# Two transformer blocks in one kernel: the first projections of the neighbourhood attention behind the last state product

## The chip, the cores and the metric

The kernel runs on one core of one Trainium2 chip. The metric is the device time of one execution in microseconds (us), the median of several runs. Besides it there is one profiled execution, from which all rows below come.

## What is computed

The reference runs two different transformer blocks in turn on 256 tokens of width 1024. Each has two layers. In the first block a layer mixes tokens by three branches: a latent attention (mla), a gated linear attention (gla) and a neighbourhood attention (na). Its input is 256 tokens and 256 context tokens. In the first layer context tokens are also given out, so all 512 tokens pass through; in the second only 256 outputs are needed, though keys and values of all 512 are.

```python
def hybrid_layer(h, hc, ...):
    z = modulate(rms_norm(h, norm1_w), sh1, sc1) @ w_in
    zc = modulate(rms_norm(hc, norm1_w), csh1, csc1) @ w_in
    a, bb, cc, gates = split_cols(z, GROUP_SPLITS)
    ya, ya_c = mla_mixer(a, a_c, ...)
    yb, yb_c = gla_mixer(bb, bb_c, ...)
    yc, yc_c = na_mixer(cc, cc_c, na_rpb, need_ctx_out)
    h = h + g1 * merge_branches(ya, yb, yc, gates, w_a_o, w_b_o, w_c_o, w_out)
    h = h + g2 * swiglu(...)

def gla_mixer(...):
    ...
    def finish(o, g):
        o = rms_norm(o.transpose(0, 2, 1, 3), norm_w)
        b, l = o.shape[0], o.shape[1]
        return o.reshape(b, l, GLA_V_W).astype(g.dtype) * jax.nn.silu(g)
```

The three branches read the same normed input. So the projections of the neighbourhood attention don't depend on what the linear attention gives.

## The kernel before

The program is written engine by engine. Each of TensorE (`pe`), ScalarE (`act`), VectorE (`dve`), GpSimd (`pool`) and SyncE (`sp`, which starts the transfers) has its own list of instructions, by hand, and semaphores between them. `x_done.at(label)` is the count of engine x at which a step with that label is over. `stage(...)` at the head of a part makes an engine wait until all four have ended the part before.

**Matmuls.** Matrices are kept as a high and a low part, and a product is three matmuls (high by high, high by low, low by high). `three`, lines 566 to 568, does it for projections that give features by tokens; `v_part`, lines 1213 to 1215, gives tokens by features.

**Weight panels.** All weights go through the same three raw buffers, in one fixed order, as panels of up to 128 x 2048. For each panel SyncE loads `raw` (line 516). `step(p)` prepares panel p + 2: ScalarE copies it to the high part `whi` (534); then VectorE takes the low part `wlo` of 5/8 of the columns and GpSimd that of the rest (543). `open_panel` on TensorE waits for all three, and `panel_used` counts the panels that TensorE is through with. A raw buffer is free for the next transfer once both low parts are made. In layer 0 panels of the modulation weights `w_mod` go through the same raw buffers. They aren't split; TensorE multiplies them as they are (line 770), and the last 17 of them stand in the neighbourhood attention of layer 0.

**The linear attention's end.** It runs over 8 chunks of 64 tokens, forward and then backward. In each step VectorE updates the state (2407), and TensorE makes an outer product (1158) and the product with the state (1190), which adds into the output in banks 0 to 3. OT is the number of token blocks of 128 that are given out, 4 in layer 0 and 2 in layer 1. In the backward pass the first 2 x OT steps also hold a gate product each (745 to 747). Ahead of these steps VectorE masks the products within a chunk (2393). ScalarE takes the silu of the gates (1803). After the last product with the state it squares the output and sums each head (1811), and takes the root (1814). VectorE inverts it (2413), norms (2417), multiplies with the gate (2422). TensorE turns each token block by four matmuls with the identity (894), and VectorE copies it to `y` (2423). The turned blocks use banks 6 and 7 in turn.

**The neighbourhood attention's beginning.** Panel 0 holds queries and keys of two heads (48 matmuls with up to 512 columns), panel 1 the values of four heads (96 matmuls with 256 columns, four token blocks). Then an attention loop over heads and query blocks starts with the score products (1237). The other projections are cut into parts, called fills, and laid into its steps by `na_plan`. SyncE loads a bias table `nbias` in 12 transfers (2895), GpSimd masks it in four operations (2775, 2778), and VectorE adds it to the scores (2142) and takes their maximum (2156). In the program of before, the bias transfers wait for the end of the linear attention on all four engines, and stand ahead of panel 2 in SyncE's list. GpSimd masks ahead of its share of panels 2 and 3.

## Time and profile before

| what | us |
|---|---|
| median of 3 runs | 3116.35 |
| lowest, highest | 3114.63, 3122.04 |
| the profiled execution | 3119.45 |
| its span, first to last instruction | 3117.7 |
| TensorE busy, matmuls | 2812.8 (90%) |
| mean granted TensorE clock | 0.951 |

TensorE is the busiest engine by far; VectorE is busy for 44% of the span, ScalarE for 39%, GpSimd for 36%. A share of the whole span says little about one seam between two stages, though: what counts there is who waits for whom, in order of time. The granted clock is a share of full speed: 1.00 is 2.4 GHz, 0.50 is 1.2 GHz.

### The profile page before, as it was taken

How to read it: one execution, taken by the hardware profiler on the slowest of the kernel's cores; microseconds unless marked ns; L12 is line 12 of the kernel's file. 1: busy time of each engine (PE TensorE's matmuls, PEld its weight loads, DVE VectorE, ACT ScalarE, POOL GpSimd, SP SyncE). 2: the span in 40 equal slices, each digit the busy share in tenths (PEclk: the TensorE clock that was granted, in tenths of full speed). 3: DMA queues.
4: the chain of work that ended last, by engine and by line, in shares of the span. 5: the costliest groups of instructions: out<-in, count | busy, mean ns of one | idle time of the engine just before them, and what ended most of it. 6: DMA issues, size and time to landing. Idle time of an engine off the chain costs nothing. (4 is left out here: it accounts for less than half of the span.)

```text
span 3117.7 us, 52810 instructions
## 1 busy us (share of the span) xinstructions
PE 2812.8 (90%) x20541; PEld 2502.8 (80%) x20541; DVE 1359.5 (44%) x2405; ACT 1217.7 (39%) x1791; POOL 1117.6 (36%) x457
## 2 busy tenths in 40 slices
PE   6789879799889999888789899899889999988998
PEld 4557667588779999566679799899779989977898
DVE  2443533332343433444434543534564353456433
ACT  2322223333244444422345444444444444444443
POOL 0101020132235565111214455354425555632453
PEclk8899989899989999998999999999999999989999
DMA  5454034533336666211415566465225646622563
GB/s 173 131 180 147 14 83 127 156 91 104 94 109 192 188 194 191 83 29 41 88 48 152 164 197 189 141 198 165 95 82 162 188 138 197 190 84 68 149 186 97
DMA packets 570660, 413.54 MB, mean 133 GB/s; under 512 B 36566, under 2 KB 548252, under 8 KB 570524
## 3 DMA queue, kind: packets, MB, share of 16 engines
q1 hardware_dynamic: 570524, 411.69, 44.6%
q8 instruction: 91, 1.49, 0.2%
q14 instruction: 45, 0.37, 0.0%
HBM read 410.58 MB, written 2.88 MB: 133 GB/s over the span
## 5 line engine op out<-in xcount | busy, mean ns | idle before, releaser
L543 POOL TENSOR_TENSOR wlo<-raw,whi 128x768 fp32r<-128x768 f32 (+2 forms) x353 | 1020.3, 2894 | 1701.6 <-ACT whi L534 1701.2
L566 PE MATMUL psum<-xh_n,whi 128*128 128x256 f32 (+1 forms) x3208 | 932.3, 291 | 79.6 <-DVE rtmp L2612 21.7
L567 PE MATMUL psum<-xl_n,whi 128*128 128x256 f32 (+1 forms) x3208 | 915.1, 285 | 0.0
L568 PE MATMUL psum<-xh_n,wlo 128*128 128x256 f32 (+1 forms) x3208 | 914.7, 285 | 0.0
L543 DVE TENSOR_TENSOR wlo<-raw,whi 128x1280 fp32r<-128x1280 f32 (+2 forms) x353 | 531.2, 1505 | 665.3 <-ACT whi L534 665.1
L534 ACT ACTIVATE whi<-raw 128x2048 fp32r<-128x2048 f32 (+2 forms) x353 | 643.2, 1823 | 396.0 <-PE psum L925 171.8
L566 PEld LDWEIGHTS psum<-xh_n,whi 128*128 128x128 f32 x3208 | 615.4, 192 | 114.4 <-issue 57.7
L568 PEld LDWEIGHTS psum<-xh_n,wlo 128*128 128x128 f32 x3208 | 617.3, 192 | 5.5
L567 PEld LDWEIGHTS psum<-xl_n,whi 128*128 128x128 f32 x3208 | 616.4, 192 | 4.7
L923 PE MATMUL psum<-hidh,whi 128*128 128x256 f32 x1232 | 344.0, 279 | 7.0 <-issue 7.0
L925 PE MATMUL psum<-hidh,wlo 128*128 128x256 f32 x1232 | 343.6, 279 | 0.0
L924 PE MATMUL psum<-hidl,whi 128*128 128x256 f32 x1232 | 343.6, 279 | 0.0
L923 PEld LDWEIGHTS psum<-hidh,whi 128*128 128x128 f32 x1232 | 234.1, 190 | 7.5 <-issue 7.5
L925 PEld LDWEIGHTS psum<-hidh,wlo 128*128 128x128 f32 x1232 | 234.7, 191 | 0.0
L924 PEld LDWEIGHTS psum<-hidl,whi 128*128 128x128 f32 x1232 | 234.1, 190 | 0.0
L1653 ACT ACTIVATE sg<-psum 128x256 f32<-128x256 f32 x154 | 59.2, 385 | 420.5 <-PE psum L568 420.4
L2201 DVE TENSOR_TENSOR hidf<-sg,psum 128x256 f32<-128x256 f32 x154 | 64.8, 421 | 259.9 <-ACT sg L1653 259.7
L566 PE MATMUL psum<-xh,whi 128*128 128x512 f32 (+1 forms) x360 | 146.1, 406 | 23.2 <-ACT whi L534 19.9
L567 PE MATMUL psum<-xl,whi 128*128 128x512 f32 (+1 forms) x360 | 143.3, 398 | 0.0
L568 PE MATMUL psum<-xh,wlo 128*128 128x512 f32 (+1 forms) x360 | 142.8, 397 | 0.0
L566 PEld LDWEIGHTS psum<-xh,whi 128*128 128x128 f32 (+1 forms) x360 | 68.9, 191 | 44.5 <-issue 19.0
L2203 DVE TENSOR_TENSOR hidl<-hidf,hidh 128x256 fp32r<-128x256 f32 x154 | 70.6, 458 | 74.6 <-ACT hidh L1655 74.6
(337 smaller groups left out, 3804.3 us busy)
## 6 DMA issues: line engine op xcount, KB each, us to landing
raw<-in_ffn_w_in SPq DMA_DIRECT2D x176, 512.0 KB
raw<-in_w_in SPq DMA_DIRECT2D x136, 512.0 KB
raw<-in_w_ffn_in SPq DMA_DIRECT2D x132, 512.0 KB
raw<-in_w_mod SPq DMA_DIRECT2D x96, 512.0 KB
raw<-in_ffn_w_out SPq DMA_DIRECT2D x88, 512.0 KB
raw<-in_w_ffn_out SPq DMA_DIRECT2D x66, 512.0 KB
raw<-in_w_out SPq DMA_DIRECT2D x32, 512.0 KB
raw<-in_w_a_o SPq DMA_DIRECT2D x16, 256.0 KB
```

The costliest lines, as they stand in the source:

```text
L534: act.activation(whi[slot][:, 0:size], raw[r % 3][:, 0:size], ACT.Copy).then_inc(hi_ready, 1)
L543: eng.tensor_tensor(wlo[slot][:, c0:c1], raw[raw_at[p0] % 3][:, c0:c1], whi[slot][:, c0:c1].bitcast(F32), ALU.subtract).then_inc(sem_, 1)
L566: pe.matmul(dst, sh, mh, start=start and n == 0, stop=False, skip_group_check=True)
L567: pe.matmul(dst, sh, ml, start=False, stop=False, skip_group_check=True)
L568: last = pe.matmul(dst, sl, mh, start=False, stop=n == len(pairs) - 1, skip_group_check=True)
L923: pe.matmul(dst, hi[:, w0:w0 + P], hidh[:, s_, j, :], start=False, stop=False, skip_group_check=True)
L924: pe.matmul(dst, hi[:, w0:w0 + P], hidl[:, s_, j, :], start=False, stop=False, skip_group_check=True)
L925: m = pe.matmul(dst, lo[:, w0:w0 + P], hidh[:, s_, j, :], start=False, stop=False, skip_group_check=True)
L1653: act.activation(sg[:, c, :], bank[4 + c][:, 0:S], ACT.Silu).then_inc(silu_done, 1)
L2201: dve.tensor_tensor(hidf[:, c, :], sg[:, c, :], bank[4 + c][:, S:2 * S], ALU.mult).then_inc(hid_done, 1)
L2203: dve.tensor_tensor(hidl[:, s_, c, :], hidf[:, c, :], hidh[:, s_, c, :].bitcast(F32), ALU.subtract).then_inc(hid_lo, 1)
```

## The change

It moves work at the seam between the linear and the neighbourhood attention, in both layers. No matmul is added or left out.

- TensorE: panel 0 (queries and keys, now into banks 4 and 5) stands directly behind the last state product. Then token blocks 0 and 1 of the linear attention's output are turned, then comes token block 0 of the values, then the other output blocks are turned, and then value blocks 1 to 3. The values go to banks 0 to 3, so each waits until the output in its bank is normed. The `stage` wait between the two attentions is gone on all engines.
- ScalarE: the high part of panel 0 is made ahead of the silus, that of panel 1 between the silus and the squares, and that of panel 3 behind the first value block.
- VectorE: its share of panel 0 stands behind the fourth state update of the backward pass, that of panel 1 behind the last. The key copy stands ahead of panel 2's share.
- GpSimd: its share of panel 2 stands ahead of the bias masks.
- SyncE: the transfer of panel 2 stands ahead of the bias transfers, which now wait only for the last state product.
- Memory: `nbias` lies behind what the linear attention still uses, `gst` has a place of its own, and the other small tiles are laid so that they cover only what is dead.

```diff
@@ memory
-        gst, o = at(o, "gst", [P, 16])
+        gst, _ = at(scratch + 33 * 1024, "gst", [P, 16])
...
-        nbias, o = at(o, "nbias", [P, HEADS, 6, 64])
...
+        nbias, o = at(scratch + 34 * 1024, "nbias", [P, HEADS, 6, 64])
@@ TensorE
-                pe.wait_ge(*act_done.at((tg, "silu", OT - 1)))
-                turn_y((tg, "y"), range(OT), lambda i: gv[:, i, :])
-                end("pe", tg)
...
-                stage(pe, "pe", tg, ("gla", l))
...
+                def v_head(t):
+
+                    if t < OT:
+                        pe.wait_ge(*dve_done.at((of_gla, "gn", t)))
+                    m = v_part(p0 + 1, t, 0, 8, bank[t][:, 0:S])
...
+                open_panel(pe, p0)
+                qk_part(p0, 0, slice(0, TM), 0, 8, bank[4][:, 0:TM]).then_inc(*pe_done.tick((tg, "mm", "q", 0)))
+                qk_part(p0, 1, slice(0, T), 0, 8, bank[5]).then_inc(panel_used, 1)
+                pe.wait_ge(*act_done.at((of_gla, "silu", OT - 1)))
+                turn_y((of_gla, "y"), (0, 1), lambda i: gv[:, i, :])
+                open_panel(pe, p0 + 1)
+                v_head(0)
+                turn_y((of_gla, "y"), range(2, OT), lambda i: gv[:, i, :])
+                end("pe", of_gla)
+                for t in range(1, 4):
+                    v_head(t)
@@ GpSimd
+                step(p0)
                 pool.wait_ge(*bias_loaded.at(("bias", l)))
-                pool.wait_ge(lo_ready_pool, p0 + 2)
+                pool.wait_ge(lo_ready_pool, p0 + 3)
...
-                for j in range(6):
+                for j in range(1, 6):
                     step(p0 + j)
@@ SyncE
-                for s_ in (pe_done, act_done, dve_done, pool_done):
-                    sp.wait_ge(*s_.at(("end", ("gla", l))))
+                sp.wait_ge(*pe_done.at(((("gla", l), "b"), "from state", 7)))
...
-                before[base["na", l] + 2] = [lambda l=l: bias_loads(l)]
+                before[base["na", l] + 3] = [lambda l=l: bias_loads(l)]
```

On TensorE, at the seam of layer 0, the program of before has this (`whi_54` and `wlo_57` are panel 0's parts, `whi_52` and `wlo_55` panel 1's):

```order
1023 L1190 MATMUL psum<-state,qdec 64x256 x2
1024 L894 MATMUL psum<-cst,gv 128x128 x16
1025 L566 MATMUL psum<-xh,whi_54 128x512
...
1073 L1213 MATMUL psum<-whi_52,xh 128x256
...
1169 L1237 MATMUL psum<-nk,nq 128x512 x2
```

and the changed one this:

```order
1023 L1190 MATMUL psum<-state,qdec 64x256 x2
1024 L566 MATMUL psum<-xh,whi_54 128x512
...
1072 L894 MATMUL psum<-cst,gv 128x128 x8
1073 L1209 MATMUL psum<-whi_52,xh 128x256
...
1097 L894 MATMUL psum<-cst,gv 128x128 x8
1098 L1209 MATMUL psum<-whi_52,xh 128x256
...
1170 L1243 MATMUL psum<-nk,nq 128x512 x2
```

The 16 turning matmuls (line 894) stood ahead of both panels; now eight stand behind panel 0 and eight behind the first value block.

On ScalarE at the same place, before (`whi_53` is panel 2's high part, and the later `whi_54` panel 3's):

```order
113 L1797 ACTIVATE kend<-psum 128x256 x4
114 L1803 ACT_TABLE_LOAD
115 L1803 ACTIVATE la<-psum 128x512 x4
116 L1811 ACTIVATE expc,gst<-psum 128x128 x16
117 L1814 ACT_TABLE_LOAD
118 L1814 ACTIVATE gst<-gst,eps 128x16
119 L534 ACTIVATE whi_54<-raw_49 128x2048
120 L534 ACTIVATE whi_52<-raw_50 128x2048
121 L534 ACTIVATE whi_53<-raw_51 128x2048
122 L1829 ACTIVATE nq<-psum 128x512
```

and now:

```order
113 L1803 ACTIVATE kend<-psum 128x256 x4
114 L534 ACTIVATE whi_54<-raw_49 128x2048
115 L1810 ACT_TABLE_LOAD
116 L1810 ACTIVATE la<-psum 128x512 x4
117 L534 ACTIVATE whi_52<-raw_50 128x2048
118 L1819 ACTIVATE expc,gst<-psum 128x128 x16
119 L1822 ACT_TABLE_LOAD
120 L1822 ACTIVATE gst<-gst,eps 128x16
121 L1834 ACTIVATE nq<-psum 128x512
122 L534 ACTIVATE whi_53<-raw_51 128x2048
```

Panel 0's high part moved ahead of the silus, panel 1's between silus and squares, and panel 2's behind the query copy.

On VectorE the changed program has, from the masked copies on:

```order
275 L2399 COPY_PREDICATED attm<-cst,psum 128x2x128 x8
276 L2413 SCALAR_TENSOR_TENSOR state<-state,expc,psum 64x128 x16
277 L543 TENSOR_TENSOR wlo_57<-raw_49,whi_54 128x1280
278 L2413 SCALAR_TENSOR_TENSOR state<-state,expc,psum 64x128 x12
279 L543 TENSOR_TENSOR wlo_55<-raw_50,whi_52 128x1280
280 L2422 RECIPROCAL gst<-gst 128x16
```

Before, the 28 state operations stood in one row, and both low parts behind the last copy of the turned output.

## Rows read from the trace of the kernel before

**Rows 1.** The page: the span, and GpSimd's share of a panel's low part.

```profile
span 3117.7 us, 52810 instructions
...
L543 POOL TENSOR_TENSOR wlo<-raw,whi 128x768 fp32r<-128x768 f32 (+2 forms) x353 | 1020.3, 2894 | 1701.6 <-ACT whi L534 1701.2
```

**Rows 2.** Busy time by stretch, layer 0: PE, PEld, DVE, ACT, POOL, clock, DMA, GB/s.

```profile
380.00:416.20 36.20, 36.20 (x286) 30.11 (x284) 9.70 (x28) 2.39 (x4) 0.00 (x0) 1.00 0.00 1
416.20:436.00 19.80, 4.14 (x17) 3.00 (x16) 12.36 (x27) 9.77 (x36) 4.26 (x2) 0.58 0.00 0
436.00:448.70 12.70, 12.66 (x48) 10.38 (x49) 1.19 (x1) 0.00 (x0) 1.71 (x1) 0.85 1.21 194
```

**Rows 3.** TensorE's waits, 416.2 to 461: total us, times, longest.

```profile
PE psum L894 <- DVE gv L2422: 9.8, 2, 8.7
PE psum L894 <- DVE y L2423: 3.6, 1, 3.6
PE psum L566 <- DVE wlo L543: 2.4, 1, 2.4
```

**Rows 4.** Order of time, seam of layer 0: start, us, instruction [idle before <-releaser].

```profile
415.12 1.08 PE L1190 MATMUL psum<-state,qdec 128*64 128x256 f32 x4
...
416.24 0.28 ACT L1811 ACTIVATE expc<-psum 128x128 f32<-128x128 f32 x1 [0.41 <-PE psum L1190]
...
422.44 3.69 ACT L534 ACTIVATE whi<-raw 128x2048 fp32r<-128x2048 f32 x2
...
424.92 1.09 PE L894 MATMUL psum<-cst,gv 128*128 128x128 f32 x4 [8.71 <-DVE gv L2422]
...
425.84 1.16 DVE L2422 TENSOR_TENSOR gv<-gv,la 128x512 f32<-128x512 f32 x1
...
430.90 1.28 DVE L2423 COPY y<-psum 128x512 f32<-128x512 f32 x2
...
434.31 2.88 DVE L543 TENSOR_TENSOR wlo<-raw,whi 128x1280 fp32r<-128x1280 f32 x2
```

**Rows 5.** Order of time, layer 0: TensorE from the projections on, and SyncE's next request.

```profile
440.82 0.39 PE L567 MATMUL psum<-xl,whi 128*128 128x512 f32 x1
...
448.75 0.28 PE L1213 MATMUL psum<-whi,xh 128*128 128x256 f32 x1
...
460.99 1.13 PE L1237 MATMUL psum<-nk,nq 64*128 64x512 f32 x4 [0.57 <-ACT nv L1836]
...
461.36 8.85 SPq L516 DMA_DIRECT2D raw<-in_w_mod  x6
...
466.68 1.07 PE L770 MATMUL psum<-raw,cpad 128*32 128x256 f32 x16 [1.61 <-DMA raw<-in_w_mod]
```

**Rows 6.** Order of time, layer 0: the bias table, and a split beside it.

```profile
434.53 8.13 SPq L2895 DMA_DIRECT2D nbias<-bias_bands  x12
...
446.99 2.45 POOL L2775 TENSOR_SCALAR_AFFINE_SELECT nbias<-nbias 64x2304 f32<-64x2304 f32 x1 [18.32 <-DMA nbias<-bias_bands]
...
454.77 3.51 POOL L2778 TENSOR_SCALAR_AFFINE_SELECT nbias<-nbias 64x2304 f32<-64x2304 f32 x1
...
452.30 3.66 DVE L543 TENSOR_TENSOR wlo<-raw,whi 128x1280 fp32r<-128x1280 f32 x1 [15.11 <-ACT whi L534]
```

**Rows 7.** Order of time, VectorE, backward pass of layer 0: masked copies, a state update.

```profile
374.70 1.44 DVE L2393 COPY_PREDICATED attm<-cst,psum 128x256 f32<-128x256 int32 x4
...
398.88 1.43 DVE L2407 SCALAR_TENSOR_TENSOR state<-state,expc,psum 64x128 f32<-64x128 f32 x4 [3.23 <-PE psum L1190]
```

**Rows 8.** Order of time, the seam of layer 1.

```profile
1511.91 1.08 PE L1190 MATMUL psum<-state,qdec 128*64 128x256 f32 x4 [0.52 <-DVE state L2407]
...
1520.22 1.16 DVE L2422 TENSOR_TENSOR gv<-gv,la 128x512 f32<-128x512 f32 x1
...
1547.11 1.13 PE L1237 MATMUL psum<-nk,nq 64*128 64x512 f32 x4 [0.57 <-ACT nv L1836]
...
1550.01 0.36 PE L566 MATMUL psum<-xh_n,whi 128*128 128x256 f32 x1 [1.77 <-POOL wlo L543]
```

38 lines of the change are left out of this document (16 added, 22 removed).

## The prediction

> **What bounds the kernel now.** I first looked at the whole run: one core, a span of 3117.7 us [rows 1]. Then I went to the place that the change touches, the seam between the linear attention and the neighbourhood attention, which occurs once per layer. The stretch view shows the seam of layer 0 [rows 2]: TensorE is busy throughout the 36.2 us before it, works 4.1 of the 19.8 us in it, and is busy again behind it. The view of who waited for whom [rows 3] splits the pause: 9.8 us for the normed output, 3.6 us for a turned block to be copied out, 2.4 us for the low part of a weight panel. VectorE, ScalarE and GpSimd are used too, but they have idle time everywhere else in the seam; so here time is what TensorE waits, and it is worth its full length because the stages on both sides are full of TensorE work.
>
> The rows of the tail [rows 4] tell why. The last state product begins at 415.12 and ends at 416.20. ScalarE then squares the output, the first turning matmul can start at 424.92, the first turned block is copied out at 430.90, behind the norm of the fourth, and only behind the last copy does VectorE make the low part of the next two panels (434.31, 2.88 us for two). The projections use none of the normed output. They wait only because they stand behind it.
>
> **Layer 0, TensorE.** The change puts the 48 matmuls of queries and keys straight behind the last state product. At full clock one with 512 columns takes (448.75 - 440.82) / 35 = 0.227 us, and one of the value part (460.42 - 448.75) / 96 = 0.12 us [rows 5], where 460.42 is 460.99 less the wait of 0.57 in front of it. The 48 take 48 x 0.227 = 10.9 us, from 416.2 to 427.1.
>
> Next come two turned blocks. ScalarE now has the high part of the value panel (3.69 / 2 = 1.85 us) between its last silu, which ended 0.41 us ahead of the squares' start, and the squares; they begin at about 417.7 instead of 416.24, and the chain behind them is 1.5 us later. Block 0 was ready for turning at 424.92, now at 426.4, before TensorE comes. Block 1 was ready at 425.84 + 1.16 = 427.0, now at 428.5. A turn takes 1.09 us: 427.1 to 428.2, a wait of 0.3, 428.5 to 429.6. The first value part (24 x 0.12 = 2.9) ends at 432.5. Blocks 2 and 3 wait for VectorE to copy blocks 0 and 1 out of the two banks, which it does behind the norm of block 3: 430.9 + 1.5 = 432.4, plus 0.65 for a copy, 433.1. So there is a wait of 0.6, then two turns to 435.3, then three value parts (8.6) to 443.9, and the same 0.57 as before to the first score product: 444.5. It stood at 460.99 [rows 5]. **Gain: 16.5 us.** Of these 1.8 are clock: in the stretch of 12.7 us with exactly these 48 matmuls the granted clock was 0.85 [rows 2]; warm they take 10.9.
>
> **Layer 0, what is late next.** The first modulation panel was waited for 1.6 us at 466.68 [rows 5]. Its transfer can only be asked for when panel 2 of this stage has been split, since it takes that buffer. Panel 2 is now transferred ahead of the bias tables and split on GpSimd ahead of the bias masks; VectorE does its share behind the last copies and the key copy, at worst in the 3.66 us of the slow row [rows 6]: 435.3 + 0.65 + 0.65 + 3.7 = 440.3. Before, the request went out at 461.36 and the panel was there 5.3 us later [rows 5]; so it lands at about 445.6, and TensorE asks 4.1 us behind the scores (466.68 - 1.61 - 460.99), at 448.6. **This wait goes: 1.6 us.**
>
> The bias must be ready too. Its first transfer was issued at 434.53 and the masks began 12.5 us later, taking 454.77 + 3.51 - 446.99 = 11.3 us [rows 6]. It now waits only for the last state product of TensorE: 416.3 + 12.5 = 428.8. GpSimd has panel 2's split in front: ScalarE is free for it at 422.44 + 1.5 = 423.9, copies the queries first (0.6) and needs 1.85, to 426.4; GpSimd adds 2.9, its mean for a share [rows 1], to 429.3. So the masks end at 440.6, 4 us before the scores. Covered. The later raw panels follow the bias as before and come earlier with it.
>
> **Layer 0, VectorE and the state products.** The low part of the first panel (1.44 us) now stands between the fourth and the fifth state update. VectorE idled 3.23 us ahead of the fifth [rows 7], so this costs nothing; in layer 1 the same part of the chain waits for TensorE too. The high part on ScalarE fills part of an idle stretch between the decay exponentials and the silu. GpSimd's share of that panel now runs while VectorE makes the masked copies, 1.44 us for two blocks [rows 7], on which TensorE does wait. GpSimd slows some VectorE work: the split, with two operands in SBUF, took 3.66 us beside the masks against 1.44 [rows 4, 6]. The masked copy has one operand in SBUF, one in PSUM, so I take 0. The upper bound: within the 2.9 us of GpSimd's work VectorE loses the same part as in the split, (3.66 - 1.44) / 3.66 = 0.61, or 1.8 us, all of it exposed. Below nothing there is no reason for a gain.
>
> The Trainium skill speaks against this step: GPSIMD Engine Reference, section Specifications, says that GpSimd's SBUF interfaces are shared with VectorE, with contention where a VectorE instruction has two SBUF inputs or uses both ports. The 3.66 us row agrees for two SBUF inputs; for masked copies no row shows it. By the rule my zero holds if the copy counts as one SBUF input; if it counts as two, both layers lose up to 1.8 us and the time is 3088.6.
>
> **Layer 1.** Only two token blocks are computed, so the query part has 256 columns: 24 x 0.12 + 24 x 0.227 = 8.3 us. The last state product ends at 1511.91 + 1.08 = 1513.0 [rows 8], so the projections run to 1521.3. Here the last gate product lies several steps before the end, so ScalarE's extra split is done before the squares. Block 1 was ready at 1520.22 + 1.16 = 1521.4. Two turns: 1523.5. Four value parts: 11.5 us, 1535.0, and 0.57: 1535.6 against 1547.11. **Gain 11.5 us.** Behind the first scores TensorE waited 1.77 us for GpSimd's share of panel 2 (the row at 1550.01), which now stands ahead of the masks. **Gain 1.8 us.** The bias: 1513.1 + 12.5 + 11.3 = 1536.9, when VectorE wants it behind the first scores, at 1535.6 + 1.1 = 1536.7. Here the cover is just used up. A small delay meets TensorE's fills: what is left of the projections, 3 x 8.3 + 11.5 = 36.4 us of matmuls, is laid over 11 steps, 3.3 us each, and TensorE asks for the first softmax after two of them. So I take 0.
>
> **Sum.** 16.5 + 1.6 + 11.5 + 1.8 = 31.4 us. The span goes from 3117.7 [rows 1] to 3086.3. The profiled execution took 3119.45 us, so it would take 3088.1. It lay 3.1 above the median of the three runs, 3116.35; from that median I get 3085.0. I expect every stage behind the seams to move rigidly, since there TensorE waited for its own work and not for transfers. A measurement can tell about 0.3% (9.3 us) from no change.
>
> **Rivals.** (A) The forecast: 3085, chance 0.66.
> (B) Bias and contention become the limit. If all four masks take the 3.51 us of the slow one, the bias of layer 1 is ready at 1539.6, 2.8 us late; with 1.8 us of slower masked copies per layer this costs up to 6.4: 3091. For it: layer 1 has no slack. Against it: the fills. 0.14.
> (C) One seam's gain is given back: a panel or modulation transfer, now asked for elsewhere, is waited for later in layer 0, where 17 modulation panels share the buffers. It would take about half: 3116.35 - 16 = 3100. Against it: the only such wait in the first steps is 1.6 us, and the requests move earlier together with the work. 0.10.
> (D) Further small waits in the first attention steps go as well: 3080. 0.05.
> (E) Slower: the clock. The stretch with 4.1 us of work had a granted clock of 0.58 and the next one 0.85 [rows 2]. If the turns, with their waits, let it fall to half at 416 and keep it there through both projections, these cost their warm length again: 10.9 + 11.5 + 8.3 + 11.5 = 42 us against 31.4 gained, 3127. It decides only if over three quarters of both projections run at half clock. Against it: the longest remaining wait is 0.6 us, while TensorE has worked for 36 us ahead. 0.02.
> The Trainium skill (TensorE: Matmul & The Clock Gate, Part 1) says that idling halves the clock and continued work gives it back; rows 2 agree, and by that rule (E) needs an idle gap that my sequence does not have.
> (F) It does not do what it says: the first panel is not ready at 416.2, and TensorE waits for it as long as before: 3116. Its transfer is long over, and the split's three shares are done in idle time. 0.03.
>
> **How the numbers follow.** The likeliest is 3085. B lies at 3091, D at 3080; the scatter of runs (3114.63 to 3122.04) adds 2 below and up to 6 above. The range 3079 to 3097 takes in A, B and D and leaves out most of C, E and F. Faster by over 0.3% is A to D: 0.95. Within: F, 0.03. Slower: E, 0.02.
>
> **What would show it.** Right: the first projection matmul of layer 0 less than 0.3 us behind the last state product, at full clock; first scores at about 28.3 us behind the end of the last state product (now 44.8), in layer 1 22.6 (now 34.1); no wait on the first modulation panel; the masks end before the first bias addition in layer 0. Wrong: a wait ahead of the fifth state update longer than before, a granted clock of 0.5 in the projections, VectorE waiting for the masks in layer 0, or a new TensorE wait for a transfer in the 100 us behind.

## The result, and the profile after

The changed kernel takes 3087.19 us (median of 4 runs, 3084.45 to 3095.62), the kernel before on the same chip 3119.19 us (4 runs, 3114.63 to 3123.0). The ratio is 0.9907, with a 95% interval of 0.9887 to 0.9926, so about 29 us or 0.9% faster. The prediction was 3085.0 us, with a range of 3079 to 3097. Two further comparisons on another chip gave 3092.27 against 3118.75 (ratio 0.9903, 0.9880 to 0.9926) and 3090.71 against 3118.42 (0.9918, 0.9890 to 0.9946). One of all runs, of the kernel with the late bias below, took 4117 us at a mean granted clock of 0.64; it is left out of every median and ratio.

The profiled execution of the changed kernel took 3087.04 us. This is the first line of its page, and it answers to [rows 1]:

```profile
span 3085.2 us, 52796 instructions
```

The span is 32.5 us shorter than the 3117.7 us of before. The two seams do not give all of that, as will be seen. First TensorE's rows from the seam of layer 0 (start in us, duration in us, engine, line, operation, count, and in brackets the idle time ahead and what ended it). They answer to [rows 4] and [rows 5]. The lines of the file have moved: the first scores are L1243 now, L1237 before.

```profile
413.96 1.08 PE L1190 MATMUL psum<-state,qdec 128*64 128x256 f32 x4
414.97 0.50 PE L566 MATMUL psum<-xh,whi 128*128 128x512 f32 x1
...
425.99 0.60 PE L894 MATMUL psum<-cst,gv 128*128 128x128 f32 x4
427.45 0.66 PE L894 MATMUL psum<-cst,gv 128*128 128x128 f32 x4 [0.86 <-DVE gv L2431]
...
433.85 1.54 PE L894 MATMUL psum<-cst,gv 128*128 128x128 f32 x8 [2.87 <-DVE y L2432]
435.61 0.41 PE L1211 MATMUL psum<-whi,xl 128*128 128x256 f32 x1
...
438.12 0.28 PE L1211 MATMUL psum<-whi,xl 128*128 128x256 f32 x1
...
445.79 1.13 PE L1243 MATMUL psum<-nk,nq 64*128 64x512 f32 x4 [0.57 <-ACT nv L1841]
```

The query and key projections (L566 and its two neighbours) start as soon as the last state product is through. From the start of that product to the first scores it takes 445.79 - 413.96 = 31.8 us, where it was 460.99 - 415.12 = 45.9. Two things in the rows are worse than forecast. The wait ahead of the last two turns is 2.87 us and not 0.6. And behind it a matmul of the value part takes 0.41 us until 438, and 0.28 from then on. The view of stretches (busy time of the engines and count, then PEclk, the granted clock) says why; it answers to [rows 2]:

```profile
414.00:426.00 12.00, 12.00 (x54) 9.51 (x54) 6.39 (x12) 10.75 (x38) 2.83 (x2) 1.00 0.95 134
426.00:434.00 8.00, 4.27 (x35) 3.86 (x34) 7.93 (x13) 2.18 (x2) 7.32 (x4) 1.00 0.99 258
434.00:436.00 2.00, 2.00 (x12) 1.82 (x12) 1.56 (x3) 0.00 (x0) 1.86 (x2) 0.65 0.03 8
436.00:438.00 2.00, 2.00 (x12) 2.00 (x11) 2.00 (x3) 0.00 (x0) 2.00 (x1) 0.50 0.01 4
438.00:445.80 7.80, 7.23 (x62) 7.06 (x61) 4.40 (x2) 1.29 (x4) 2.97 (x2) 1.00 0.69 227
```

Behind a stretch in which TensorE worked 4.27 of 8 us the clock went to its lower level for 3.4 us. Those matmuls took twice their time, which is some 1.5 us.

VectorE's rows for the same place show where the 2.87 us come from. L2426 is the norm, L2431 the multiplication with the gate, L2432 the copy of a turned block out of PSUM.

```profile
424.13 0.69 DVE L2431 TENSOR_TENSOR gv<-gv,la 128x512 f32<-128x512 f32 x1
424.74 1.12 DVE L2426 SCALAR_TENSOR_TENSOR gv<-psum,gst,gln 128x128 f32<-128x128 f32 x4
425.90 1.50 DVE L2431 TENSOR_TENSOR gv<-gv,la 128x512 f32<-128x512 f32 x1
427.32 1.11 DVE L2426 SCALAR_TENSOR_TENSOR gv<-psum,gst,gln 128x128 f32<-128x128 f32 x4
428.47 1.78 DVE L2431 TENSOR_TENSOR gv<-gv,la 128x512 f32<-128x512 f32 x1
430.18 1.11 DVE L2426 SCALAR_TENSOR_TENSOR gv<-psum,gst,gln 128x128 f32<-128x128 f32 x4
431.32 1.77 DVE L2431 TENSOR_TENSOR gv<-gv,la 128x512 f32<-128x512 f32 x1
433.02 1.28 DVE L2432 COPY y<-psum 128x512 f32<-128x512 f32 x2
```

The same multiplication takes 0.69, 1.50, 1.78 and 1.77 us, and the norm between, which reads PSUM, 1.11 or 1.12 every time. GpSimd's rows lie beside them: its share of the third attention panel (L543), then the masks on the bias (L2781, L2784).

```profile
425.02 1.83 POOL L543 TENSOR_TENSOR wlo<-raw,whi 128x768 fp32r<-128x768 f32 x1 [6.62 <-ACT whi L534]
427.25 2.46 POOL L2781 TENSOR_SCALAR_AFFINE_SELECT nbias<-nbias 64x2304 f32<-64x2304 f32 x1 [0.40 <-DMA nbias<-bias_bands]
429.86 2.70 POOL L2784 TENSOR_SCALAR_AFFINE_SELECT nbias<-nbias 64x2304 f32<-64x2304 f32 x1
432.70 2.71 POOL L2781 TENSOR_SCALAR_AFFINE_SELECT nbias<-nbias 64x2304 f32<-64x2304 f32 x1
```

Only the first multiplication meets no GpSimd instruction. The other three end 0.54 or 0.55 us behind the end of the one that ran when they started: 425.90 + 1.50 = 427.40, and the share ended at 425.02 + 1.83 = 426.85; 428.47 + 1.78 = 430.25 against 427.25 + 2.46 = 429.71; 431.32 + 1.77 = 433.09 against 429.86 + 2.70 = 432.56. So it looks as if VectorE's multiplication stood still until GpSimd's instruction was all but over. The kernel before shows the same, with two of GpSimd's shares in one row:

```profile
424.41 4.26 POOL L543 TENSOR_TENSOR wlo<-raw,whi 128x768 fp32r<-128x768 f32 x2 [96.83 <-ACT whi L534]
428.07 1.15 DVE L2422 TENSOR_TENSOR gv<-gv,la 128x512 f32<-128x512 f32 x1
```

The shares end at 428.67 and the multiplication at 429.22, 0.55 us behind. Experiments below test whether GpSimd is the cause.

In layer 1 the stretch is 1518.52 - 1496.59 = 21.9 us (before 1547.11 - 1511.91 = 35.2, [rows 8]). GpSimd's last two masks, TensorE's first scores and VectorE's first use of the bias:

```profile
1515.00 3.79 POOL L2781 TENSOR_SCALAR_AFFINE_SELECT nbias<-nbias 64x2304 f32<-64x2304 f32 x1
1518.93 2.45 POOL L2784 TENSOR_SCALAR_AFFINE_SELECT nbias<-nbias 64x2304 f32<-64x2304 f32 x1
...
1518.52 1.13 PE L1243 MATMUL psum<-nk,nq 64*128 64x512 f32 x4 [0.56 <-ACT nv L1841]
...
1521.41 0.43 DVE L2148 TENSOR_TENSOR psum<-psum,nbias 128x256 f32<-128x256 f32 x1 [4.94 <-POOL nbias L2784]
```

The first scores start at 1518.52, and VectorE adds the bias to them only at 1521.41, since the masks end at 1521.38. What followed from that is in the view of TensorE's waits from 1496 to 1535 (total, times, longest):

```profile
PE psum L1243 <- ACT npr L1639: 1.1, 1, 1.1
PE psum L1243 <- ACT nv L1841: 0.6, 1, 0.6
```

The new wait of 1.1 us is for the softmax behind the late bias, and at 1530.3 the clock fell to half speed for some 3 us. So the 1.77 us that TensorE no longer waits for GpSimd's share [rows 8] went back within this attention: from first to last scores it takes 69.9 us, before 69.6. The wait is the smaller part of that. TensorE is busy for 68.0 us of this attention, and in the kernel before for 66.6 of its own, so the lower clock costs 1.4 us.

### The profile page after: what moved, and what is told of

It reads as the page before. It is cut to its first block and busy times, and to the rows that moved or that the text cites. A ratio compares the mean times of both kernels' runs of the same rounds, so it can differ in the third digit from the quotient of the medians.

```text
span 3085.2 us, 52796 instructions
## 1 busy us (share of the span) xinstructions
PE 2800.3 (91%) x20541; PEld 2493.7 (81%) x20541; DVE 1364.3 (44%) x2405; ACT 1217.5 (39%) x1791; POOL 1116.4 (36%) x457
## 5 line engine op out<-in xcount | busy, mean ns | idle before, releaser
L543 POOL TENSOR_TENSOR wlo<-raw,whi 128x768 fp32r<-128x768 f32 (+2 forms) x353 | 1018.1, 2887 | 1703.6 <-ACT whi L534 1703.2
L566 PE MATMUL psum<-xh_n,whi 128*128 128x256 f32 (+1 forms) x3208 | 933.0, 291 | 75.8 <-DVE rtmp L2618 21.8
L543 DVE TENSOR_TENSOR wlo<-raw,whi 128x1280 fp32r<-128x1280 f32 (+2 forms) x353 | 531.7, 1507 | 641.3 <-ACT whi L534 641.1
L566 PEld LDWEIGHTS psum<-xh_n,whi 128*128 128x128 f32 x3208 | 615.9, 192 | 109.7 <-issue 55.1
L566 PE MATMUL psum<-xh,whi 128*128 128x512 f32 (+1 forms) x360 | 145.4, 404 | 20.8 <-ACT whi L534 19.9
L566 PEld LDWEIGHTS psum<-xh,whi 128*128 128x128 f32 (+1 forms) x360 | 68.6, 191 | 42.0 <-issue 16.6
```

The lines of the kernel that those rows point to most:

```text
L543: eng.tensor_tensor(wlo[slot][:, c0:c1], raw[raw_at[p0] % 3][:, c0:c1], whi[slot][:, c0:c1].bitcast(F32), ALU.subtract).then_inc(sem_, 1)
L566: pe.matmul(dst, sh, mh, start=start and n == 0, stop=False, skip_group_check=True)
```

## Experiments

The table is the key to all of them. A stretch runs from the start of the last state product to the start of the first scores; "attention" is from there to the start of the last scores. Both are differences of start times of TensorE's rows in the profiled execution. The last columns are medians of runs, of the kernel and of the kernel before on the same chip; the first row has the median of the four runs beside the changed kernel's first.

| kernel | stretch, layer 0 | attention 0 | stretch, layer 1 | attention 1 | median | before |
|---|---|---|---|---|---|---|
| before | 45.9 | 126.5 | 35.2 | 69.6 | 3119.2 | |
| changed | 31.8 | 126.1 | 21.9 | 69.9 | 3087.2 | 3119.2 |
| changed, second profile | 31.8 | 127.9 | 21.9 | 69.6 | 3092.3 | 3118.8 |
| changed, third profile | 31.8 | 127.8 | 21.9 | 69.6 | 3090.7 | 3118.4 |
| TensorE's order back | 42.7 | 127.9 | 31.9 | 69.4 | 3116.7 | 3123.4 |
| bias late | 38.3 | 132.5 | 31.7 | 71.9 | 3118.3 | 3123.4 |
| panel share and transfer behind the bias | 31.9 | 128.0 | 24.5 | 72.4 | 3100.5 | 3118.8 |
| copies early | 31.2 | 126.3 | 22.0 | 69.7 | 3099.4 | 3123.4 |
| GpSimd quiet | 27.3 | 130.0 | 21.9 | 69.7 | 3097.7 | 3123.4 |
| bias early | 28.1 | 128.0 | 21.9 | 67.7 | 3081.8 | 3118.8 |
| bias early, again | 28.1 | 127.8 | 22.0 | 67.7 | 3087.8 | 3118.4 |
| bias and copies early | 28.1 | 127.8 | 21.9 | 67.7 | 3089.2 | 3118.8 |
| bias early and GpSimd quiet | 27.3 | 126.2 | 21.9 | 69.3 | 3082.5 | 3118.4 |

The stretches of one kernel agree within 0.1 us. Attention 0 is either about 126.2 or about 127.9, in the same kernel too, and that is the clock. In the changed kernel's second and third profile it fell for another 3.4 us, some 10 us behind the first scores; in its first it stayed up there. Here are 3.4 us of the second profile, with 14 matmuls:

```profile
457.20:460.60 3.40, 3.40 (x14) 2.33 (x16) 0.86 (x2) 0.17 (x1) 0.00 (x0) 0.50 1.00 333
```

and the same place of the first, with 27:

```profile
455.70:459.10 3.40, 2.85 (x27) 1.76 (x26) 1.28 (x3) 1.57 (x4) 0.00 (x0) 1.00 1.05 341
```

The waits ahead of it are the same in all three (1.27 us for VectorE's sums). Profiles of 127.8 to 128.0 us all have this fall and those of 126.1 to 126.5 don't. The totals differ by 15 us and more from run to run; so verdicts rest on the stretches, and totals are compared only as medians of runs taken together.

### TensorE's order put back

Arguments and waits are left out here:

```
-                qk_part(...); turn_y(..., (0, 1), ...); v_head(0); turn_y(..., range(2, OT), ...); v_head(1..3)
+                turn_y((of_gla, "y"), range(OT), lambda i: gv[:, i, :])
+                qk_part(...); v_head(0..3)
```

> Only TensorE's order goes back: it turns all blocks first and runs the projections behind them; ScalarE, VectorE, GpSimd and SyncE keep the changed order. The stretch is counted from the start of the last state product to the start of the first scores (before 45.9 us in layer 0 and 35.2 in layer 1; changed 31.8 and 21.9). Theory I (the gain is TensorE working during the norm): TensorE stands idle again for some 11 us behind the state product, and the stretches come back to 42 to 46 us and 32 to 35, total near 3113 us. Rival R (the gain is mainly the earlier splits and the earlier bias on the other engines): the stretches stay under 36 and 26, total under 3098.

Measured: 42.7 and 31.9 us (the latter just under the 32 to 35 expected), median 3116.67 us against 3123.42 of before (ratio 0.9979, 0.9953 to 1.0004). Theory I holds. TensorE's rows in layer 0:

```profile
413.42 1.08 PE L1190 MATMUL psum<-state,qdec 128*64 128x256 f32 x4
424.43 1.08 PE L894 MATMUL psum<-cst,gv 128*128 128x128 f32 x4 [9.93 <-DVE gv L2429]
426.10 1.12 PE L894 MATMUL psum<-cst,gv 128*128 128x128 f32 x4 [0.59 <-DVE gv L2429]
430.32 1.94 PE L894 MATMUL psum<-cst,gv 128*128 128x128 f32 x8 [3.10 <-DVE y L2430]
```

The waits for the normed output are back: 9.93 + 0.59 = 10.5 us, 9.8 in [rows 3]. What the other engines' new order is worth alone is 45.87 - 42.74 = 3.1 us and 35.20 - 31.93 = 3.3 us; the wait of 2.4 us for a low part [rows 3] is gone with it. TensorE's order is worth the other 10.9 and 10.0. The stretch in layer 0 also has turns of 1.08 us, where the changed kernel has 0.60: they are the same matmuls at the lower level of the clock (0.50 from 424.4 to 434) and at the higher.

### Bias transfers late

```
-                sp.wait_ge(*pe_done.at(((("gla", l), "b"), "from state", 7)))
+                for s_ in (pe_done, act_done, dve_done, pool_done):
+                    sp.wait_ge(*s_.at(("end", ("gla", l))))
```

> The changed kernel, but the bias transfers of each layer wait again until all four engines are through with the linear attention. Theory I (the order of TensorE and the earlier bias are both needed): the first scores start where they do in the changed kernel (31.8 and 21.9 us behind the last state product), but VectorE then waits for the masks, since transfers of 8 us, their landing and masks of 11 us stand behind the last turned copy: 8 to 14 us in layer 0 and 10 to 14 in layer 1, total 3105 to 3112. Rival R (the bias is covered anyway): VectorE waits under 2 us more in each layer, total 3087 to 3092.

Measured: 38.3 and 31.7 us, attentions 6 and 2 us longer, median of nine runs 3118.29 us (ratio 0.9992, 0.9967 to 1.0018), where 3105 to 3112 was expected. The early bias is needed, as theory I has it, but the mechanism is another than I wrote, and the loss is larger: the first scores themselves came late, and VectorE then waited only 2.35 us for the masks in layer 0. SyncE's queue, ScalarE and TensorE in layer 0:

```profile
432.78 8.13 SPq L2901 DMA_DIRECT2D nbias<-bias_bands  x12
441.01 4.48 SPq L516 DMA_DIRECT2D raw<-in_w_in  x4
...
448.37 1.91 ACT L534 ACTIVATE whi<-raw 128x2048 fp32r<-128x2048 f32 x1 [17.95 <-DMA raw<-in_w_in]
450.19 0.91 ACT L1841 ACTIVATE nv<-psum 128x256 f32<-128x256 f32 x3
...
451.25 1.22 PE L1243 MATMUL psum<-nk,nq 64*128 64x512 f32 x2 [10.70 <-ACT nv L1841]
```

The transfer of a weight panel stands behind the bias in SyncE's queue; ScalarE waits 17.95 us for that panel, and behind its split stand three copies of values (L1841) that the first scores wait for. A late request costs whatever is queued behind it, on its own queue and then on the engine that waits for the next item. Of the 27 us that the changed kernel's seams gain, this one edit gives back 6.5 us and 4.6 to 6.4 (attention 132.5 against 126.1 to 127.9) in layer 0, and 9.8 and 2 in layer 1.

### GpSimd's panel share behind the masks, its transfer behind the bias

```
-                step(p0)
                 pool.wait_ge(*bias_loaded.at(("bias", l)))
...
-                for j in range(1, 6):
+                for j in range(6):
...
-                before[base["na", l] + 3] = [lambda l=l: bias_loads(l)]
+                before[base["na", l] + 2] = [lambda l=l: bias_loads(l)]
```

> The changed kernel with GpSimd's masks ahead of its share of the third attention panel and the bias transfers ahead of that panel's load, as in the kernel before. Theory I (the share of 1.8 us stands behind 10 to 11 us of masks): in layer 0 the masks still start some 12 us behind the state product and the panel is whole at about 25, when TensorE reaches it; in layer 1 TensorE waits 1 to 4 us for the panel ahead of the first fill, the stretch to the scores as changed (31.8, 21.9 within 1 us); total 1 to 5 us over the changed kernel. Rival R (the order on GpSimd is indifferent): total within 1 us, no wait of TensorE for the panel.

Measured: 31.9 and 24.5 us, median 3100.50 us beside 3092.27 us for the changed kernel. The seam of layer 0 is as expected in length, with one wait of 3.76 us between the turns in place of 0.86 and 2.87. In layer 1 the stretch was expected within 1 us of 21.9 and came out 2.6 longer. TensorE waits twice:

```profile
1532.18 2.08 PE L1243 MATMUL psum<-nk,nq 64*128 64x512 f32 x4 [3.01 <-ACT nv L1841]
1535.45 0.55 PE L566 MATMUL psum<-xh_n,whi 128*128 128x256 f32 x1 [1.19 <-POOL wlo L543]
```

The second wait is the one expected, the first (2.4 us over the usual 0.57) is again ScalarE behind a panel that landed later. ScalarE waited 11.31 us for panel 2, whose transfer stood behind the twelve of the bias, and 2.78 us for panel 3 behind it, and the copies of values stand behind that split. So the first wait points to SyncE's order and only the second to GpSimd's. Stretch and attention together are 2.6 + 2.5 = 5.1 us longer, all of it in layer 1. The edit puts both orders back, and how the 5.1 us divide between them isn't shown. The median is 8.2 us over the changed kernel's, more than the 1 to 5 expected; the part above 5.1 is within the scatter of runs.

### Copies early: is it VectorE's order?

```
                     dve.tensor_tensor(gv[:, i, :], gv[:, i, :], la[:, i, :], ALU.mult).then_inc(...)
-                turn_evac((tg, "y"), range(OT), ...)
+                    if i >= 2:
+                        copy_turned(i - 2)
+                for i in range(OT - 2, OT):
+                    copy_turned(i)
```

> The changed kernel, but VectorE copies turned block i-2 out right behind the gate multiply of block i (layer 0 has four blocks, layer 1 two, where nothing changes), so that the copy that TensorE's third turn waits for stands ahead of the last multiply. Theory I (the 2.9 us wait of the turns is VectorE's order behind multiplies that take 1.8 us beside GpSimd, and it halves the granted clock): the wait falls under 1.5 us, the clock stays at 1.0 to the first scores, and layer 0's stretch falls from 31.8 to 28.5 to 30 us. Rival R (the clock falls at any wait there, or the wait is due to the multiplies' time and not to the order): wait over 2 us or clock 0.5 again, stretch 31 to 32.5. The total moves 1 to 3 us, less than runs differ by.

Measured: wait 2.22 us (now ahead of the fourth turn, for the copy of block 1), granted clock 0.70 from 434 to 438, stretch 31.2 us. That is the rival. The order is worth 0.65 us of the 2.87; what holds the copy back are the multiplications ahead of it.

### GpSimd quiet beside the multiplications

```
+                pool.wait_ge(*dve_done.at(((("gla", l), "y"), "ready", mix_tokens(l) // P - 1)))
                 step(p0)
                 pool.wait_ge(*bias_loaded.at(("bias", l)))
```

> The changed kernel, but GpSimd's share of the third attention panel and the masks wait until VectorE has multiplied the last block by its gate, so that VectorE's four multiplies run with GpSimd still. Theory I (GpSimd slows them): all four multiplies of layer 0 take 0.7 us each (changed: 0.69, 1.50, 1.78, 1.77), TensorE's wait for the turned copy falls from 2.9 to under 1 us, the clock stays up; but the masks end 7 to 8 us later and VectorE waits for them, 1 to 4 us in layer 0 and 1 to 8 in layer 1: total 3087 to 3097. Rival R (they are slow for another reason, such as reading a PSUM bank or waiting for TensorE): the multiplies still take 1.5 to 1.8 us.

Measured: all four multiplications 0.69 us, stretch 27.3 us in layer 0.

```profile
416.90 1.08 PE L1190 MATMUL psum<-state,qdec 128*64 128x256 f32 x4
428.93 1.31 PE L894 MATMUL psum<-cst,gv 128*128 128x128 f32 x8
433.81 1.23 PE L894 MATMUL psum<-cst,gv 128*128 128x128 f32 x8 [0.69 <-DVE y L2432]
```

```profile
433.70:438.00 4.30, 4.19 (x35) 4.04 (x36) 4.09 (x5) 1.78 (x2) 3.93 (x3) 1.00 0.54 169
```

The wait is 0.69 us, near the 0.6 of the prediction, and the clock stays up behind it. So GpSimd's work beside VectorE's multiplications is the cause of 4.5 us in this stretch (31.8 - 27.3): 3.0 of them are the three slower multiplications and 1.5 the clock behind the wait. But the masks now end 6.6 us later; VectorE waits for them (4.94 us ahead of its first bias addition), and TensorE 3.4 us, in place of 1.27, for a modulation sum behind that. The attention takes 130.0 us. The clock also fell in it, from 455.2, so it is to be set against the 127.9 of the changed kernel with such a fall: some 2.1 of the 4.5 us go back. In layer 1 nothing is lost, because there the transfer of the bias, and not GpSimd, sets when the masks start.

### Bias early: both causes away

```
-        kinv, o = at(o, "kinv", [P, 2, T])
         kend, o = at(o, "kend", [P, 4, S])
+        kinv, o = at(o, "kinv", [P, 2, T])
...
-                for j in range(7):
+                for j in range(6):
...
-                step(p0)
                 pool.wait_ge(*bias_loaded.at(("bias", l)))
-                pool.wait_ge(lo_ready_pool, p0 + 3)
+                pool.wait_ge(lo_ready_pool, p0 + 1)
...
-                for j in range(1, 6):
+                step(p0 - 1)
+                end("pool", gla_tg)
+                for j in range(6):
...
-                sp.wait_ge(*pe_done.at(((("gla", l), "b"), "from state", 7)))
+                sp.wait_ge(*pe_done.at(((("gla", l), "b"), "att", mix_tokens(l) // P - 1)))
```

The bias lay over kend, which the state chain reads to its end. With kend and kinv exchanged it lies over kinv, which is read last by the masked products, some 36 us earlier.

> The changed kernel with two tiles of the linear attention exchanged (kend below kinv), so that the bias lies over tiles that the masked products have read last; its transfers start behind those products, some 35 us before the last state product, and GpSimd masks before its last share of the linear attention's panels and its share of the third attention panel. Theory I (masks beside the gate multiplies slow these; a late bias costs layer 1 some 2 us): masks end before the last state product, multiplies 0.7, at most one of 1.5 beside the panel share, TensorE's wait 0.7 us, clock 1.0, the first scores 27 to 28.5 us (layer 0) and 21.9 us (layer 1) behind the state product, no wait of VectorE for masks in either (changed: 4.9 us in layer 1), total 5 to 7 us under the changed kernel. Rival R (masks now slow the state chain, which TensorE waits for): the state products take longer by the same 2 to 5 us, total no better.

Measured: 28.1 and 21.9 us, no wait for masks, attention 1 67.7 us in place of 69.6, median 3081.78 us beside 3092.27. The stretches are as expected; the 10.5 us between the medians are more than the expected 5 to 7, which is why the kernel was run again below. The masks of layer 0 run deep in the state chain; this is the first, and the last ends at 402.59:

```profile
391.31 2.45 POOL L2780 TENSOR_SCALAR_AFFINE_SELECT nbias<-nbias 64x2304 f32<-64x2304 f32 x1 [13.87 <-DMA nbias<-bias_bands]
```

The rival's price isn't there: from the last masked product to the last state product it takes 36.3 us in this kernel and in the changed one, and 22.6 in layer 1. TensorE's waits between the turns, from the view of 412 to 456:

```profile
PE psum L894 <- DVE gv L2431: 0.9, 1, 0.9
PE psum L894 <- DVE y L2432: 0.7, 1, 0.7
```

One expectation missed: in layer 1 the masks ended 1.5 us behind the start of the last state product and not ahead of it. Nobody waits for them there.

The 1.9 us of attention 1 are mostly clock again. TensorE's waits for softmaxes there are 0.4 and 0.6 us, in the changed kernel 1.1 and 0.6 or 0.8 and 0.6, and its busy time is 66.4 us in place of 68.0: the fall of the clock behind the late softmax is gone. The last kernel below shows that the fall isn't tied to the late bias alone.

The same kernel again, beside a third measurement of the changed one:

> The kernel with the early bias once more, against the changed kernel on the same chip. By its seams it gains 3.7 us in layer 0 and 1.9 us in layer 1's attention, so 5.6 us: theory I expects a median 3 to 9 us under the changed kernel, stretches 28.1 and 21.9 us. Rival R (the 10.5 us of the last comparison are an effect of its own elsewhere): median 10 us or more under it again.

Measured: 3087.82 us beside 3090.71, with the stretches as before (28.1, 22.0, 67.7). The 2.9 us are just short of the 3 to 9 that I gave. The 12 runs of this kernel together have a median of 3083.8 us, the 13 of the changed kernel on that chip 3090.8: 7 us, near the 5.6 that the seams give (3.7 + 1.9).

### Bias and copies early

> The early bias and the early copy-out of the turned blocks together. Theory I: once the multiplies take 0.7 us the order of the copies hardly matters: stretches within 0.5 us of the early bias alone, total within 2 us of it. Rival R (VectorE's order matters by itself): TensorE's last turns start 0.7 us or more earlier than with the early bias alone, stretch 26.5 us in layer 0.

This is the early bias with the edit of the early copies on top. Measured: 28.1, 21.9 and 67.7 us, each within 0.1 of the early bias alone. TensorE waits 0.85 us for the copy of block 1 in place of 0.69 for block 0. The order of the copies is worth nothing once the multiplications take 0.7 us. The median of 3089.24 us is 7.5 over that of the early bias alone, where 2 at most was expected, with stretches and attentions that agree. The ratios to before overlap (0.9873 to 0.9925, and 0.9860 to 0.9913), and three feed-forward stages of this profile ran at the slower of the two paces told of below, so I take the 7.5 us for scatter.

### Early bias with GpSimd quiet

```
                 step(p0 - 1)
                 end("pool", gla_tg)
+                pool.wait_ge(*dve_done.at(((("gla", l), "y"), "ready", mix_tokens(l) // P - 1)))
                 for j in range(6):
```

> The early bias, and GpSimd's share of the third attention panel held until VectorE has multiplied the last block by its gate, so that no GpSimd work lies beside the multiplies of either layer. Theory I (GpSimd's share slows the second multiply from 0.69 to 1.50 us in layer 0 and from 0.69 to 1.35 in layer 1): all multiplies 0.69 us, TensorE's wait between the turns 0, stretch 27.3 us in layer 0, 21.9 in layer 1, total 0.8 us under the early bias alone, less than runs differ by. Rival R (the panel comes too late for the first fill, or VectorE's own shares now meet GpSimd's): a wait of TensorE for the panel of 1 to 6 us behind the first scores in one layer, total no better.

Measured: all multiplications 0.69 us, stretches 27.3 and 21.9 us, median 3082.46 us. TensorE's wait between the turns is 0.7 and not 0, since the copy-outs still stand behind the last norm. In this profile attention 1 took 69.3 us, where the early bias alone had 67.7 twice. The clock fell once in the 30 us behind the first scores (0.94, against 1.00 there), behind the same two waits of 0.4 and 0.6 us that the early bias alone has. Busy time is 67.9 us against 66.4, which is the difference. So a fall of 1.5 us also comes without a late bias: it was there in all three profiles of the changed kernel, in none of the three with the bias early and GpSimd free to run, and in this one. I count 0.8 us in layer 0 as shown and leave the rest open. Medians lie 36 us under before here and 37 and 31 for the early bias alone, where the changed kernel has 26.5 to 32.0.

### The same kernel three times

> The changed kernel once more, beside the other three and the kernel before on one chip. The seams are rigid: the first scores again 31.8 us (layer 0) and 21.9 us (layer 1) behind the start of the last state product, each within 0.3 us, the clock at half speed for 3 to 4 us in layer 0. Theory S (the 5 us by which the profiled gain exceeds what the two seams give is scatter of the second block's feed-forward stages, whose matmuls come every 0.113 or 0.118 us from execution to execution): this profile has another mix of the two paces, and the median gain over before is 27 us, give or take 4. Rival (the change speeds those stages up): they come at the same pace as in the first profile, and the median gain stays at 32 or more.

> The changed kernel a third time, as the base for the next two. Theory S (the seams are rigid, the feed-forward stages come at one of two paces by chance): stretches 31.8 and 21.9 us again within 0.1, while the 500-matmul stretches of the feed-forward stages take 56.7 or 58.9 us, in other stages than in the two profiles of this kernel before. Rival: one of the two profiles is repeated.

Measured: stretches 31.8 and 21.9 us in all three profiles, gains in the median of 32.0, 26.5 and 27.7 us. The rest of the run isn't rigid. In the feed-forward stages TensorE is busy without a gap at full clock and still has two paces. The stretch view counts its matmuls; this is the first profile of the changed kernel:

```profile
1830.00:1880.00 50.00, 50.00 (x427) 50.00 (x426) 18.50 (x21) 21.40 (x21) 27.32 (x10) 1.00 0.63 189
2420.00:2460.00 40.00, 40.00 (x355) 40.00 (x355) 15.13 (x19) 17.77 (x20) 22.35 (x8) 1.00 0.63 191
```

and this the second, of the same program:

```profile
1830.00:1880.00 50.00, 50.00 (x443) 50.00 (x443) 18.51 (x21) 21.44 (x21) 29.39 (x10) 1.00 0.66 198
2430.00:2470.00 40.00, 40.00 (x342) 40.00 (x341) 14.16 (x16) 16.25 (x16) 22.59 (x8) 1.00 0.63 184
```

50 us hold 427 matmuls in one and 443 in the other, 0.117 and 0.113 us each, and 600 us later it is the other way round. One stage keeps its pace to its end; 500 matmuls take 56.7 or 58.9 us, and a stage on the slower pace costs about 6 us. The kernel has seven long stages of this kind, and each was met on the slower pace in some profile of this study: one stage in the first profile of the changed kernel, another one in the second and the third, none in the first profile of the early bias and three in its second (spans 3077.5 and 3096.1 us). My expectation that the third profile would differ from both others in this failed, since it had the slow stage of the second; its span was still 12 us shorter (3086.6 against 3098.7). Theory S holds otherwise, and the total of one profile can't be used to weigh an edit of 5 us.

## Why the prediction was right, and where it was not

**The mechanism held.** TensorE's pause was waiting for work that the projections don't need. They start 1.0 us behind the start of the last state product, at full clock; with TensorE's order put back 10.9 and 10.0 us of the stretches return. The other signs of being right came too: VectorE's idle time ahead of the fifth state update is 1.68 us and not longer than the 3.23 of before, the masks of layer 0 end at 438.01, 9 us before the first bias addition, and no new wait of TensorE for a transfer stands in the 100 us behind. That the stages behind move rigidly can't be read from totals, since their pace changes from one execution to the next.

**The sum was 4 to 5 us too high, and scatter hid it.** Forecast were 31.4 us. The seams and attentions give (45.9 - 31.8) + (126.5 - 126.1) + (35.2 - 21.9) + (69.6 - 69.9) = 14.1 + 0.4 + 13.3 - 0.3 = 27.5 us. With the second and third profile, in which the clock fell once more in attention 0, it is 26.0 and 26.1. The other 5 us of the 32.5 in span came from elsewhere. One feed-forward stage lost 6.2 us at the slower pace and the last ones won 5.4, where before had run at it; these nearly cancel, and the rest is many small pieces whose causes aren't shown (1.2 us of it lies ahead of the first seam). The three measured gains, 32.0, 26.5 and 27.7 us, lie around these sums. So the nearness of 3087.19 to 3085.0 is partly luck. Term by term:

- **Layer 0's seam, 16.5 forecast, 14.1 measured.** From the end of the last state product to the first scores I had 28.3 us, and it took 445.79 - 413.96 - 1.08 = 30.8. The step that failed is "So there is a wait of 0.6". I took VectorE's norm chain with the durations of before, only shifted by 1.5 us. But the change also moved GpSimd's panel share and masks into that chain. Rows of before showed this price. The split of 452.30 took 3.66 us against 1.44 [rows 4, 6]; a mask started at 452.17, and with the usual 2.45 us it ended at 454.62, 1.34 us before the split did: the same standing still. The multiplication itself took 1.16 us in [rows 4], beside a share of GpSimd's, and 0.69 in the changed kernel with GpSimd still. I used the split's row for VectorE's part of panel 2, and for masked copies as a share of lost time, where nothing came of it; I never put it to the multiplications, as a wait to the end of GpSimd's instruction. The wait was 2.87 us. The one ahead of block 1's turn was 0.86 in place of 0.3, but for another reason: block 1 was ready 13.4 us behind the start of the last state product, as forecast (428.5 - 415.12), and TensorE was there sooner, since a turn is shorter than I took it for. With GpSimd quiet the stretch is 27.3 us from the start of the product, 26.2 from its end, 2.1 better than my sum.
- **The clock.** Rival (E) said that the turns' waits might cost clock, and set against it that the longest remaining wait is 0.6 us. It was 2.87, and the clock fell: for 3.4 us, not through both projections, at 1.5 us and not 42. The mechanism of the rival was real and its size was not. Without the wait (GpSimd quiet) the clock stays at 1.00 up to the first scores. What I had not thought of are further falls of 3.4 us in the attentions, at 1.5 to 1.7 us each.
- **A turn, 1.09 us forecast.** It takes 0.52 to 0.66 us at the higher level of the clock, and 1.54 for the two behind the long wait. The turns of before ran at the lower level; I took their duration into a sequence that runs at the higher one, while I did use warm durations for the projections. This is 4 x 1.09 - 0.60 - 0.66 - 1.54 = 1.6 us in layer 0 and 2 x 1.09 - 1.03 = 1.15 in layer 1 to the good. It is most of why **layer 1's seam** gave 13.3 instead of 11.5 us, and it hid part of the miss in layer 0.
- **The modulation panel, 1.6 us.** The wait is gone: the first of its matmuls starts 449.79 - 445.79 = 4.0 us behind the scores with nothing in brackets, against 5.7 before [rows 5]. But TensorE then waits 1.27 + 0.55 us for VectorE's copy of the sums (L759), where before it waited 0.55 alone, so by 461 most of it is given back. It was a cost in one place that the next dependence also had; only 0.3 to 0.4 us stayed.
- **GpSimd's share of panel 2 in layer 1, 1.8 us.** The wait at the first fill is gone: it starts 1.1 us behind the first scores, before 2.9 [rows 8]. The late bias and the clock took the time back. I had it ready at 1536.9 against 1536.7 wanted and took 0 for the difference. It was ready 1521.38 - 1497.67 = 23.7 us behind the end of the last state product (forecast 23.9, so right), but it was wanted at 22.0 and not at 23.7, because the projections were through earlier. "Here the cover is just used up" was right too, but the step to "So I take 0" was not: the 1.7 us of lateness met a wait of TensorE of 1.1 us and then a fall of the clock. Putting share and transfer back behind the bias costs 5.1 us, of which GpSimd's share is only a part.
- **Masked copies beside GpSimd, 0 forecast.** Right: with GpSimd's 1.81 us beside them they took 1.44 us for four and 0.78 for two, as before. 

The Trainium skill speaks of this at two places. GPSIMD Engine Reference, section Specifications, ties the contention to VectorE instructions with two SBUF inputs or in a two-port mode. For two SBUF inputs the runs agree wherever they can be read: the multiplication of two SBUF tiles is held up, while norm, copies and state update, each of which reads PSUM, keep their time beside the same work. SBUF — State Buffer, section "SBUF: two separate sides", calls the shared ports an exclusive lock that the first comer holds for its whole instruction. The ends of the three multiplications, 0.54 or 0.55 us behind the end of GpSimd's instruction, agree with that. I cited the first rule for the one instruction to which it does not apply, and missed the multiplications, to which it does; with the second, [rows 6] could have been read as a wait and priced.

**Rivals.** (B), bias and contention as the limit at 3091 us, was real in kind: 4.5 us of contention and clock in layer 0 and some 2 us in layer 1, of late bias and of the clock behind it. The second and third measurement, 26.5 and 27.7 us, are nearer to its 25 than to the 31.4 of (A). (C), something given back later, happened to most of the 1.6 and to the 1.8 us, not to half of a seam. (D) and (F) did not happen.

## What to carry to other kernels

When a change pulls independent work into a pause, write down what each of the other engines does in that pause afterwards, and price its instructions again with their new neighbours: a duration from the old trace holds only for the neighbours and the clock level that it had there. Follow a late request along its own queue and on to whoever stands behind it there, since that, and not its direct user, decided the cost of a late bias. And where stages elsewhere have two paces, judge an edit of 5 us by the stretch between two instructions around it; three profiles of one kernel agreed within 0.1 us there, while their spans differed by 13.5. Look up the granted clock in each stretch that you compare: a fall of 3.4 us is worth some 1.5 us, and it came and went between executions of one program.

## What the runs showed of the hardware

- A VectorE multiplication of two SBUF tiles of 128x512 takes 0.69 us alone. If a GpSimd instruction runs when it starts, it ends 0.54 or 0.55 us behind the end of that instruction: 1.35 and 1.50 us beside the subtraction of 128x768, 1.77 and 1.78 beside affine selects on 64 partitions, and 1.15 and 1.16 beside the subtraction in the kernel before. With the panel share behind the masks one took 2.68 us: it started 0.3 us behind a select of 2.45. GpSimd is held up the same way; selects of 2.70 and 3.5 to 3.8 us stand where VectorE's multiplication or split ran at their start. The norm (1.11 us for four), the copy from PSUM (0.64) and the state update (1.43 for four) keep their time beside the same work.
- Pauses of TensorE of 2.87 and of 2.22 us between the turns were followed by a fall of the granted clock to 0.50 for some microseconds; pauses of 0.86 and 0.69 us at the same place were not. The length of a pause doesn't settle it: behind the same 1.27 us in attention 0 the clock fell in the second and third profile of the changed kernel and not in its first, and behind the same 0.4 and 0.6 us in attention 1 it fell in the kernel with early bias and GpSimd quiet and not with the early bias alone. Each of these falls cost 1.5 to 1.7 us.
- Back-to-back matmuls with 256 columns at a granted clock of 1.00 have two paces, 0.113 and 0.118 us (56.7 and 58.9 us for 500), and a stage keeps the one it has. The records that were read show nothing that sets them apart: granted clock, TensorE's busy share and order of work are the same. What sets it stays open.
